# Attention stage of a decoder step: memory laid out anew, key pages and masks in another order, and ten places moved in the mixer

## What is computed

```python
# mixer, per head and chunk: three products in float32 and a decaying state
A = einsum('bhtd,bhsd,bhtsd->bhts', qc, kc, decay)
o = einsum('bhts,bhsv->bhtv', A, vc) + einsum('bhtd,bhdv->bhtv', qc * exp(b), S)
S = exp(b_last) * S + einsum('bhsd,bhsv->bhdv', kc * exp(b_last - b), vc)

# attention of the samples: 512 past keys from 4 pages each, 64 new ones with a mask
s_past = einsum('bqhd,bkhd->bhqk', q, k_past) * SCALE + (cq[..., :, None] - c_past[..., None, :])
s_new  = einsum('bqhd,bkhd->bhqk', q, k_new)  * SCALE + (cq[..., :, None] - cq[..., None, :])
p = softmax(concatenate([s_past, where(tri, s_new, -inf)]))
```

## Time and profile before

| | |
|---|---|
| time, median of 3 runs | 1660.13 us (1658.66 to 1663.81) |
| the profiled execution | 1661.83 us, its span 1660.2 us |
| TensorE busy | 1612.0 us (97%) |
| VectorE busy | 872.9 us (53%) |
| ScalarE busy | 627.3 us (38%) |
| GpSimd busy | 295.9 us (18%) |
| mean granted TensorE clock | 0.986 of full speed |

### The profile page before, as it was taken

The page is one execution under the profiler, slowest core; times in us unless marked ns, Lnnn a source line. Parts: engine busy times, 40 slices in busy tenths (PEclk is TensorE's granted clock), DMA queues, the critical chain, the costliest instruction groups (busy, mean ns, idle before and its releaser), DMA issues. The chain is left out here.

```text
span 1660.2 us, 36461 instructions
## 1 busy us (share of the span) xinstructions
PE 1612.0 (97%) x14334; PEld 1539.0 (93%) x14334; DVE 872.9 (53%) x1522; ACT 627.3 (38%) x995; POOL 295.9 (18%) x356
## 2 busy tenths in 40 slices
PE   7999999979999999999999999898999999999997
PEld 7999999969999999999999999655899999999997
DVE  5667666645555555432354444666555555554221
ACT  6344444323333333322244455655443333333110
POOL 1222222222222222100100100222122222221000
PEclk9999999979999999999999999999999999999999
DMA  5222222212222222322233433688422222223330
GB/s 201 68 89 80 79 79 79 79 54 82 84 81 88 76 81 84 88 80 83 79 115 123 139 98 96 241 310 303 164 73 87 86 76 88 76 88 92 97 96 31
DMA packets 52164, 173.97 MB, mean 105 GB/s; under 512 B 7074, under 2 KB 8626, under 8 KB 52066
## 3 DMA queue, kind: packets, MB, share of 16 engines
q1 hardware_dynamic: 47138, 155.45, 29.3%
q0 software_dynamic: 4928, 17.12, 2.9%
HBM read 159.98 MB, written 12.57 MB: 104 GB/s over the span
## 5 line engine op out<-in xcount | busy, mean ns | idle before, releaser
L1537 PE MATMUL acc<-xl,w_hi 128*128 128x288 f32 x2160 | 478.6, 303 | 9.9 <-DVE w_lo L990 9.9
L1537 PE MATMUL acc<-xh,w_lo 128*128 128x288 f32 x2160 | 464.8, 297 | 0.0
L1537 PE MATMUL acc<-xh,w_hi 128*128 128x288 f32 x2160 | 464.7, 297 | 0.0
L806 DVE TENSOR_TENSOR w_lo<-w_raw,w_hi 128x1024 fp32r<-128x1024 f32 (+1 forms) x215 | 281.6, 1310 | 333.0 <-ACT w_hi L440 331.9
L1537 PEld LDWEIGHTS acc<-xl,w_hi 128*128 128x128 f32 x2160 | 349.4, 190 | 19.2 <-DVE w_lo L990 9.9
L1537 PEld LDWEIGHTS acc<-xh,w_hi 128*128 128x128 f32 x2160 | 350.3, 190 | 0.0
L1537 PEld LDWEIGHTS acc<-xh,w_lo 128*128 128x128 f32 x2160 | 349.9, 190 | 0.0
L440 ACT ACTIVATE w_hi<-w_raw 128x1024 fp32r<-128x1024 f32 (+1 forms) x215 | 222.5, 1035 | 316.0 <-PE acc L1537 284.0
L1537 PE MATMUL acc<-ffn_glo,w_hi 128*128 128x288 f32 x704 | 151.1, 296 | 0.0
L1537 PE MATMUL acc<-ffn_gh,w_lo 128*128 128x288 f32 x704 | 149.8, 293 | 0.0
L1537 PE MATMUL acc<-ffn_gh,w_hi 128*128 128x288 f32 x704 | 148.9, 293 | 0.0
(11 more groups left out here) (264 smaller groups left out, 2150.4 us busy)
## 6 DMA issues: line engine op xcount, KB each, us to landing
w_raw<-w_fi_in SPq DMA_DIRECT2D x88, 512.0 KB, 3.5
w_raw<-w_fo_in SPq DMA_DIRECT2D x32, 512.0 KB, 3.5
att_Kd<-cache_k_in SPq DMA_DIRECT2D x32, 512.0 KB, 5.3
att_Vd<-cache_v_in SPq DMA_DIRECT2D x32, 512.0 KB, 5.8
w_raw<-w_mix_in SPq DMA_DIRECT2D x31, 512.0 KB, 3.6
w_raw<-w_o_in SPq DMA_DIRECT2D x16, 512.0 KB, 3.5
w_raw<-w_kv_in SPq DMA_DIRECT2D x16, 512.0 KB, 3.6
w_raw<-w_qg_in SPq DMA_DIRECT2D x16, 512.0 KB, 3.5
```

The source lines that it names most:

```text
L806: nc.vector.tensor_tensor(w_lo[:, pos.slot % SPL, 0:width], w_raw[:, pos.slot, 0:width], w_hi[:, pos.slot % SPL, 0:width].bitcast(F32), AL ...
L1537: mm = nc.tensor.matmul(dst[:, hf, 0:HALF], W[:, sp_, 128 * (j0 + j):128 * (j0 + j) + 128], X[:, kt, HALF * hf:HALF * hf + HALF], start=(f ...
```

## The change

1. **Mixer.** Ten entries of the table `quarters` move to a later key tile: gram 2 from j = 3 to 4 and gram 3 from 5 to 6 in quarter 0; gram 4 from 0 to 1, gram 5 from 3 to 4 and gram 6 from 6 to 7 in quarter 1; gram 7 from 1 to 2, the second `state` from 0 to 2 (now behind gram 7), `turn_v` from 4 to 5 and `turn_k` from 6 to 7 in quarter 2; `ds` from 1 to 2 in quarter 3. No step is added or taken away.
2. **Memory.** `Kd` moves over `xh` and `xl`, which are free during the query stage; `PT`, `PTd`, `Og`, `B` and `NC0` move over `x2h` and `x2l`, which are free after it. `sqq` now lies over the second half of `Pr`.
3. **SyncE.** The first sample's key pages are fetched during the query stage, behind the second `NC` and ahead of the four `w_o1` blocks. The first `B` and the mask `own` come after `block_done` B_WO1, ahead of the first value pages.
4. **GpSimd.** For i = 0 the masks come as 0, 1, (wait for B_WO1) 3, 2, and then the zeroing of `PTd`, the queries and the own mask. `mx(0, 1)` waits for two masks and no longer for three.
5. **Sample scores.** Keys and bias of a sample lie as 512 past and 64 new columns, where they lay as two halves of 256 and 32. Sixteen matmuls for each sample instead of 32; the row `c_samp` is written by two DMAs instead of three, the copies and exponentials take one run of 576 columns.

```diff
-        sqq = Region("qgs", t3.at)("sqq", [P, 2, T], F32R)
-        PT = t3("PT", [P, 2, 2, NCH, P])
+        Kd = t3("Kd", [P, PAGES, 8 * P])
...
+        PT = t4("PT", [P, 2, 2, NCH, P])
+        PTd = t4("PTd", [P, PAGES + 1, P])
+        Og = t4("Og", [P, P]); B = t4("B", [P, T]); NC0 = t4("NC0", [P, 2, P])
...
+        def sample_bank(n):
+
+            return acc[:, unit_bank(n, 4)].rearrange("p a n -> p (a n)")[:, 0:T]
...
             key_bias(1, 1)
-            sp.wait_ge(cs_dram, 48)
-            sample_bias(0)
+            key_pages(0)
             for j in range(4):
                 load(Pos(B_WO1 + j), d["w_o1"][j])
             sp.wait_ge(block_done, B_WO1)
-            key_pages(0)
+            sp.wait_ge(cs_dram, 32)
+            sample_bias(0)
+            sp.dma_start(own[:].rearrange("p n s -> p (n s)"), d["att_masks"][:, P:P + NSEQ * NS]).then_inc(ld_mask, 16)
             value_pages(0)
...
-                dve.wait_ge(msk_ok, 4 * i + (1, 3, 4, 4)[s])
+                dve.wait_ge(msk_ok, 4 * i + (1, 3 if i else 2, 4, 4)[s])
...
                 mask(i, 0)
-                mask(i, 3)
+                if i:
+                    mask(i, 3)
                 mask(i, 1)
-                if i == 0:
+                if i:
+                    sample_queries(i)
+                    mask(i, 2)
+                else:
+                    pool.wait_ge(block_done, B_WO1)
+                    mask(i, 3)
+                    mask(i, 2)
+                    nc.gpsimd.memset(PTd[:], 0.0).then_inc(kn_in, 1)
+                    pool.wait_ge(kn_in, 2)
                     pool.wait_ge(kn_ok, 16)
-                sample_queries(i)
-                mask(i, 2)
+                    sample_queries(i)
+                    pool.wait_ge(ld_mask, 48)
                 own_mask(i)
...
-                    {2: [(rec, grams_01), (tail, outs)], 3: [(rec, lambda: gram(hd, rp, 2))], 5: [(rec, lambda: gram(hd, rp, 3))],
-                     6: [(tail, onorm)]},
+                    {2: [(rec, grams_01), (tail, outs)], 4: [(rec, lambda: gram(hd, rp, 2))],
+                     6: [(rec, lambda: gram(hd, rp, 3)), (tail, onorm)]},
...
+                for new in range(2):
+                    for e in range(2):
+                        for g in range(4):
+                            p, r = 2 * g + e, slice(32 * g, 32 * g + 32)
+                            keys = KT[:, p, SEQ:T] if new else Kd[:, :, P * p:P * p + P]
+                            mm = nc.tensor.matmul(acc[r, unit_bank(n, 4), new, 0:NS if new else SEQ],
```

More of the change, by code:

```diff
@@ L406, in _ @@
             sp.dma_start(tri[:], d["att_masks"][:, 0:P]).then_inc(ld_mask, 16)
-            sp.dma_start(own[:].rearrange("p n s -> p (n s)"), d["att_masks"][:, P:P + NSEQ * NS]).then_inc(ld_mask, 16)
             sp.wait_ge(c_dram, 16)
@@ L1462, in _ @@
             pool.wait_ge(c_ok, 3)
-            for to, src in ((0, C[:, 0:256]), (256, C[:, SEQ:T]), (256 + NS, C[:, 256:SEQ])):
+            for to, src in ((0, C[:, 0:SEQ]), (SEQ, C[:, SEQ:T])):
                 pool.dma_start(d["c_samp"][:, to:to + src.shape[1]], src).then_inc(cs_dram, 16)
@@ L1466, in _ @@
             nc.gpsimd.memset(Qb[:], 0.0).then_inc(kn_in, 1)
-            nc.gpsimd.memset(PTd[:], 0.0).then_inc(kn_in, 1)
-            pool.wait_ge(ld_mask, 48)
-            pool.wait_ge(kn_in, 2)
+            pool.wait_ge(ld_mask, 32)
             def mask(i, s):
@@ L1640, in mixer @@
                 quarters = (
[L1641 to L1646 removed]
+                    {2: [(rec, grams_01), (tail, outs)], 4: [(rec, lambda: gram(hd, rp, 2))],
+                     6: [(rec, lambda: gram(hd, rp, 3)), (tail, onorm)]},
+                    {1: [(rec, lambda: gram(hd, rp, 4))], 4: [(rec, lambda: gram(hd, rp, 5)), (tail, lambda: state(0))],
+                     7: [(rec, lambda: gram(hd, rp, 6))]},
+                    {2: [(rec, lambda: gram(hd, rp, 7)), (tail, lambda: state(1))], 5: [(rec, turn_v)], 7: [(rec, turn_k)]},
+                    {2: [(rec, ds)]})
                 def run(steps):
@@ L1838, in sample_scores @@
                 pe.wait_ge(qb_ok, 2 * n + 2)
-                for hf in range(2):
-                    for new in range(2):
-                        for e in range(2):
-                            for g in range(4):
-                                p, r = 2 * g + e, slice(32 * g, 32 * g + 32)
-                                if new:
-                                    c, keys = 256 - 256 * hf, KT[:, p, SEQ + 32 * hf:SEQ + 32 * hf + 32]
-                                else:
-                                    c, keys = 32 * hf, Kd[:, 2 * hf:2 * hf + 2, P * p:P * p + P]
-                                mm = nc.tensor.matmul(acc[r, unit_bank(n, 4), hf, c:c + 256 - 224 * new],
-                                                      Qb[:, 32 * p:32 * p + 32], keys, start=(e == 0), stop=(e == 1),
-                                                      tile_position=(0, 32 * g))
+                for new in range(2):
[4 more added lines that the diff above has]
+                            mm = nc.tensor.matmul(acc[r, unit_bank(n, 4), new, 0:NS if new else SEQ],
+                                                  Qb[:, 32 * p:32 * p + 32], keys, start=(e == 0), stop=(e == 1),
+                                                  tile_position=(0, 32 * g))
                 mm.then_inc(d_ps, 1)
```

24 lines of the change are left out of this document (9 added, 15 removed).

## The result

The changed kernel takes 1650.16 us (median of four runs, 1649.78 to 1652.81) where the kernel before takes 1661.68 beside it: a ratio of 0.9935, 95% interval 0.9921 to 0.9949, which is 10.8 us (8.5 to 13.1). Measured again (first experiment) it is 0.9956 (0.9939 to 0.9973), 7.3 us (4.5 to 10.1). Either way the kernel is faster by more than its interval, and the forecast of 1.3 us was wrong.

A forecast was written before the change was run, and what follows sets the result against it. TensorE, busy 1612.0 of 1660.2 us, was taken to bound the kernel. Terms -0.8 + 0.2 + 0.4 - 0.7 - 0.4 = -1.3 us took 1660.13 to 1658.8 us; 8 in 10 range 1653.5 to 1664.

The forecast's parts named there:

- The mixer's clock: Mixer heads: half-clock spells stay at five, 0 in the sum; three to seven spells, -3.1 to +3.1 us, in the range only.
- the first rival: Mixer: a gram right behind `outs` makes the clock fall; spells go from five to one or two, -5.5 us; chance 0.10.
- Gram 2's wait: Mixer, head 1: one more key tile ahead of gram 2 covers TensorE's 0.79 us wait, -0.8 us.
- `w_lo`, +0.2: Mixer, ends of heads 2 and 3: `Vb` later, so TensorE waits about 0.1 us each for `w_lo`; between 0 and 1.2.
- the third rival: Mixer, head ends: TensorE waits for `w_lo`, slower; 1663.2 us, or 1666 with two more clock spells; chance 0.10.
- Head 8, +0.4: Mixer, head 8: gram 5 one key tile later delays VectorE's chain, which sets the end; +0.4 us, between 0 and 0.8.
- Start of the attention stage, -0.7: Before the first transposes: GpSimd's last mask starts earlier, shortening TensorE's 3.12 us wait; -0.7 us, between 0 and -1.2.
- Sample scores, -0.05 each: Attention stage: half as many matmuls, twice as wide, save some per-instruction cost; -0.4 us for eight, between +0.8 and -2.0.
- Early key pages, 0: Attention stage: sample 0's scores did not wait for keys, so fetching them early takes away no wait; 0 us.
- The period rival: Attention stage: ending the first pages' backlog removes long periods; 1654.6 us likelier, 1647 for all three; chance 0.08.

The follow-up runs named there:

- first experiment: The same changed kernel measured once more with nothing altered, against the kernel before: ratio 0.9956 (0.9939 to 0.9973).

## Why the prediction was wrong

**The mixer's clock** is the largest miss. The step that failed is "The clock I take as unchanged", a term of 0 in the sum: the ten places alone gave 5.8 us (3.3 to 8.1), of which 0.8 is the wait of head 1, and the clock's loss fell by 5.6 us, worth about 4 us at 0.7 us each. This was the first rival, held at 0.10. Its evidence for pointed the right way (gram 2 one key tile behind `outs` goes with more spells than two, 30 of 42 heads against 26 of 66). The argument against it, that `outs` is always ahead and does not move, was no argument: a cause can be needed without being enough. The forecast treated spells as noise around an unchanged mean, when the change moved that mean. The mechanism is not settled, though. The rival had gram 2 make the fall, but in head 3 of the changed kernel the clock is at half from 119.0 on, ahead of gram 2 at 121.33; in head 6 of the kernel before, too, it is at half from 240.0 on, ahead of gram 2 at 240.90. And a third key tile brought the spells back (8 of 12 heads). What is shown is a frequency, not a trigger: which of the ten places lowers it, beside a part that gram 2 seems to have, stays open. The rule quoted in the forecast from the Trainium skill ("TensorE: Matmul & The Clock Gate", What's actually happening) has the clock follow how busy TensorE has been. In the attention stage the traces agree: every spell there comes behind a wait of TensorE. In the heads they show nothing that it could go by: TensorE is busy throughout (1.00 of 119.00 to 120.00), in heads with a spell as in those without.

**Gram 2's wait, -0.8**: as forecast, gone (from head 1's first gram to head 2's it is 32.88 us, where it was 33.68).

**`w_lo`, +0.2**: did not come. `Vb` was taken to move later and came 0.9 us earlier, which cleared the way for `w_lo`. The forecast had the sign of that shift wrong; the third rival fell with it.

**Head 8, +0.4**: did not come clearly. Gram 5's take still follows at once (0.64 us behind its start, 0.65 before). From head 8's first gram to the last product of `outs` behind it, kernels have to be compared at the same clock's loss. At 3.4 us of loss the new places take 33.3 to 33.4 us and the old ones 33.1; at 5.1 us 34.0 and 34.1; at 6.8 us 35.4 and 35.7. So the term lies between +0.3 and -0.3 us.

**Start of the attention stage, -0.7**: exact at the first wait, lost by the next. TensorE's 3.12 us became 2.41, and the mask ran 1.18 us instead of 0.72 beside the key gain, as foreseen. Then VectorE's `kv_GT` took 1.28 us instead of 0.75 beside the next mask, and ScalarE's copy came late. With no spell there, as in the second measurement of the changed kernel, sample 0's scores start 14.5 us after the first mask; before it was 14.65, with a spell: at most 0.15 is left. With two adjacent spells, as in its first profile, it is 15.4, and that is no exception: seven of the fifteen profiles with the new order of masks have them, none of the five with the old one. On average over these profiles it is 14.9 us now and 14.6 before, so nothing of the 0.7 us is left. The rule of the Trainium skill that the forecast quoted ("SBUF — State Buffer", Who interferes with whom) agrees with both stretched instructions: in each pair it is the one that started later.

**Sample scores, -0.05 each**: 1131.07 + 0.41 - 1129.33 = 2.15 us, 2.19 before (the forecast's 2.17 should read 2.19).

**Early key pages, 0**: the wrong term with the subtlest reason. That the scores of sample 0 did not wait for keys was true. But the forecast priced layout, row and key pages one by one against the kernel before, and they are not separable: the layout forces `B` and `own` behind the query stage, and there only the early keys keep the queue free for them. Layout and masks alone cost 5.3 us; fetching the keys early gives 7.3 us, 5.8 of it (by the times; 4.2 of 7.9 by the profiles) by clearing the way for `B` and `own`. The sum of the attention part is 3.2 us (1.2 to 5.2) where 1.1 was forecast.

**The period rival** held part of the truth. The long periods are made by the late row, as said, and the backlog of the first pages lengthens the first long one, by some 2.5 us (18.8 against 16.3 on average), not by 4.2. That `B` would still be late stood rightly in the forecast. Only its reason, value pages issued while `B` is on its way, missed that `NC` is as late; taking away one of the two gives 0 or 3 us, both give 9. So the late row and the late `NC` together make the long periods: once neither holds the masks for long, all seven are about 14 us, in the new layout and in the old one.

**The spread.** The range of 1653.5 to 1664 came from the terms. The mixer's clock alone, bounded at 3.1 us to either side, came out at 4 to 5 on average. The bound was also too narrow for a single measurement: it counted five spells, the last at the start of head 8, while the clock's loss from there to the end of the output projection is 3.4 to 13.7 us from profile to profile. Of the distance to the first result, 1650.16 us, 2 to 3 us are luck of this kind (loss 14.0 us against 17.6 when measured again).

## What to carry over

Where two late things stand in one queue and one engine waits for both, removing one wait shows little; put them in order so that a late input holds only its own reader (here two moves gave the old kernel 12.6 us, more than the whole change). A run's mean granted clock times its span is a second measurement of every run: averaged over ten runs it showed a difference of 5.6 us in the clock's loss that no single profile can, since spells differ from run to run in heads with the same work.

## What the runs showed of the hardware

Nearly every spell took 1.7 us of clock (some 3.4 us at 0.50) and cost most heads 1.4 to 1.6 us; two to four may follow each other without a gap. In heads 2 to 7 TensorE was busy throughout when they began; in the attention stage each came behind a wait. Their frequency in the mixer depends on the order of the work (5.6 us less of clock's loss with the ten new places); their places differ between two profiles of one program. The sample scores cost nearly the same for each column with 512 columns as with 256 (from one group's start to the next 1.74 us for 16 instructions, 0.89 for 16 of half the width). Of 2.8 MB issued together (four key pages, `NC`, `B`) the last to come is used 10.4 to 13.5 us behind the first's issue (samples 1 to 6, where GpSimd waited for it): up to 13.5 in the old layout and up to 13.4 in the new one, so where the pages lie does not make it.
